# Two heads of a pair, matmul by matmul instead of head by head, in the scan of a two-block model

## The reference, cut to what matters

```python
a_cs = jnp.cumsum(a, axis=-1)
seg = a_cs[..., :, None] - a_cs[..., None, :]
decay = jnp.where(causal, jnp.exp(jnp.where(causal, seg, 0.0)), 0.0)
cb = jnp.einsum("bclgn,bcsgn->bcgls", cc, bc)
y_diag = jnp.einsum("bcgrls,bcsgrp->bclgrp", cb[:, :, :, None] * decay, xs)
...
y_off = jnp.einsum("bclgn,bcgrpn,bcgrl->bclgrp", cc, prev, jnp.exp(a_cs))
return (y_diag + y_off).reshape(b, t, h, p)
```

## Time and profile before

| what | value |
|---|---|
| median of three runs | 2549.59 us (2546.25 to 2555.57) |
| span of the profiled execution, the only time that its page gives | 2546.4 us |
| PE busy in the span | 2278.3 us (89%) |
| DVE busy | 1397.0 us (55%) |
| ACT busy | 1016.5 us (40%) |
| POOL busy | 949.7 us (37%) |
| the scan loop, four turns | 206 to 500 us of the span |
| one turn of it | 73.4 to 73.6 us |

### The profile page before, as it was taken

How to read it: one execution, slowest core, us unless ns; L and a number is a source line. 1 busy time by engine, 2 the same in 40 slices (tenths; PEclk the granted TensorE clock), 3 DMA queues, 4 the chain that set the end, 5 groups by cost and what they waited for, 6 DMA issues and landing times.

```text
span 2546.4 us, 34303 instructions
## 1 busy us (share of the span) xinstructions
PE 2278.3 (89%) x12362; PEld 1939.2 (76%) x12362; DVE 1397.0 (55%) x1514; ACT 1016.5 (40%) x1391; POOL 949.7 (37%) x253
## 2 busy tenths in 40 slices
PE   5998898878779799999789889999988988999996
PEld 3786676756658588878589879999988876778875
DVE  5637888899966433431355556306426565740633
ACT  4455555553252455542435533313223353331331
POOL 2333234336524144455432134343434223434431
PEclk9999999989889799999899889999999989999998
DMA  3232222211112122224221112222222111122221
GB/s 121 88 109 79 91 77 92 74 66 66 67 65 94 38 99 99 99 101 145 85 86 49 36 67 84 83 88 94 83 95 75 50 50 67 67 99 99 83 99 49
DMA packets 34492, 207.44 MB, mean 81 GB/s; under 512 B 4802, under 2 KB 4802, under 8 KB 10980
## 3 DMA queue, kind: packets, MB, share of 16 engines
q1 hardware_dynamic: 28128, 194.66, 21.7%
q10 hardware_dynamic: 6276, 11.57, 1.4%
HBM read 204.05 MB, written 2.17 MB: 81 GB/s over the span
## 4 chain that ended last, share of the span: by engine, by line
PE 64%; DVE 18%; DVEq 8%; ACT 4%; issue 3%; POOL 2%; ACTq 1%; DMA 0%; POOLq 0%
PE PS L505 20%; PE PS L507 19%; PE PS L509 19%; DVE vout L1578 5%; DVEq L1571 4%; POOL wlo L430 1%; PE PS L820 1%; DVEq L1474 1%; DVE hres L1475 1%; PE PS L846 1%; ACT whi L914 1%; DVE zres L1473 1%; DVE rstd L1465 1%; DVE rl L1966 1%; DVEq L1594 1%
## 5 line engine op out<-in xcount | busy, mean ns | idle before, releaser
L430 POOL TENSOR_TENSOR wlo<-raw,whi 128x2048 fp32r<-128x2048 f32 x181 | 842.2, 4653 | 1416.7 <-ACT whi L914 1398.9
L505 PE MATMUL PS<-ahi,whi 128*128 128x512 f32 (+1 forms) x2472 | 764.9, 350 | 89.4 <-DVE alo L1459 39.0
L507 PE MATMUL PS<-alo,whi 128*128 128x512 f32 (+1 forms) x2472 | 750.5, 344 | 0.0
L509 PE MATMUL PS<-ahi,wlo 128*128 128x512 f32 (+1 forms) x2472 | 748.2, 343 | 0.0
L914 ACT ACTIVATE whi<-raw 128x2048 fp32r<-128x2048 f32 x179 | 342.8, 1915 | 660.7 <-PE PS L509 655.3
L505 PEld LDWEIGHTS PS<-ahi,whi 128*128 128x128 f32 x2472 | 434.8, 193 | 165.8 <-issue 87.7
L507 PEld LDWEIGHTS PS<-alo,whi 128*128 128x128 f32 x2472 | 434.4, 192 | 52.5 <-issue 2.0
L509 PEld LDWEIGHTS PS<-ahi,wlo 128*128 128x128 f32 x2472 | 433.4, 192 | 52.6
L1578 DVE SCALAR_TENSOR_TENSOR vout<-vpad,cols,vout (+1 forms) x216 | 272.0, 1281 | 32.2 <-issue 31.6
L1966 DVE TENSOR_TENSOR rl<-rl,rstd 128x528 f32<-128x528 f32 (+1 forms) x64 | 149.0, 2328 | 248.3 <-ACT rl L1353 247.5
L505 PE MATMUL PS<-f2hi,whi 128*128 128x264 f32 (+1 forms) x768 | 205.9, 322 | 2.0 <-DVE f2lo L1972 1.8
(11 more groups left out here) (250 smaller groups left out, 2811.2 us busy)
## 6 DMA issues: line engine op xcount, KB each, us to landing
raw<-weights SPq DMA_DIRECT2D x181, 1024.0 KB, 4.8
acs_b<-acs_rows ACTq DMA_DIRECT2D x34, 256.0 KB, 3.2
const<-const ACTq DMA_DIRECT2D x2, 1232.0 KB, 6.0
x_in<-x_t SPq DMA_DIRECT2D x4, 512.0 KB, 5.2
out_t<-hres SPq DMA_DIRECT2D x8, 256.0 KB, 2.0
cols<-columns SPq DMA_DIRECT2D x1, 385.0 KB, 6.6
const<-const SPq DMA_DIRECT2D x1, 256.0 KB, 6.7
acs_rows<-dtt ACTq DMA_DIRECT2D x1, 64.0 KB
```

The lines of the kernel that those rows point to most:

```text
L430: nc.gpsimd.tensor_tensor(wlo[s][:, :], raw[s][:, :], whi[s][:, :].bitcast(F32), ALU.subtract).then_inc(lo_ready, 1)
L505: nc.tensor.matmul(o, wh, h, start=first, stop=False)
L507: nc.tensor.matmul(o, wh, h, start=False, stop=False)
L509: mm = nc.tensor.matmul(out[j], wl, hi[j], start=False, stop=last)
```

## The change: what it does

On PE, the two heads of a pair are issued together. There is one wait for `mc_ok` of both heads ahead of the pair, then for each chunk the own-chunk matmul of head 0, that of head 1, and the state matmuls of head 0 and of head 1. Both `y_mm` counts come at the end of the pair, one with the last matmul of each head. The matmuls are the same 14 per pair; their operands, places and accumulation are unchanged, and no other engine's program is changed.

```diff
-                def head(q):
-                    j, hh = q // 2, q % 2
-                    if hh == 0:
-                        hold(pe, y_ok, g * GP + max(j - 1, 0), "pe")
-                    hold(pe, mc_ok, g * GH + (q + 1), "pe")
+                def head_pair(j):
+                    hold(pe, y_ok, g * GP + max(j - 1, 0), "pe")
+                    hold(pe, mc_ok, g * GH + 2 * (j + 1), "pe")
+
+                    def out(hh, c):
+                        return PS[64 * hh:64 * hh + 64, (j % 2) * 512 + c * P:(j % 2) * 512 + (c + 1) * P]
+
+                    def cols_of(t, hh, c):
+                        q = 2 * j + hh
+                        return t[:, c * T + q * 64:c * T + q * 64 + 64]
+
                     for c in range(CHUNKS):
-                        o = PS[64 * hh:64 * hh + 64, (j % 2) * 512 + c * P:(j % 2) * 512 + (c + 1) * P]
-                        mm = nc.tensor.matmul(o, xdt[:, c * T + q * 64:c * T + q * 64 + 64],
-                                              m_slot[hh][:, c * P:(c + 1) * P], start=True, stop=(c == 0))
+                        cs = slice(c * P, (c + 1) * P)
+                        mm = [nc.tensor.matmul(out(hh, c), cols_of(xdt, hh, c), m_slot[hh][:, cs],
+                                               start=True, stop=(c == 0)) for hh in range(2)]
                         if c:
-                            mm = nc.tensor.matmul(o, st[:, (c - 1) * T + q * 64:(c - 1) * T + q * 64 + 64],
-                                                  c_slot[hh][:, c * P:(c + 1) * P], start=False, stop=True)
-                    mm.then_inc(y_mm, 1)
+                            mm = [nc.tensor.matmul(out(hh, c), cols_of(st, hh, c - 1), c_slot[hh][:, cs],
+                                                   start=False, stop=True) for hh in range(2)]
+                    for hh in range(2):
+                        mm[hh].then_inc(y_mm, 1)
...
-                head(0)
-                head(1)
+                head_pair(0)
                 z_glu(2, 0)
```

More of the change, by code:

```diff
@@ L712, in _ @@
                 hold(pe, st_ok, g + 1, "pe")
-                head(0)
-                head(1)
+                head_pair(0)
                 z_glu(2, 0)
-                head(2)
-                head(3)
+                head_pair(1)
                 z_glu(2, 1)
-                head(4)
-                head(5)
+                head_pair(2)
                 z_glu(3, 0)
-                head(6)
-                head(7)
+                head_pair(3)
                 z_glu(3, 1)
```

## The result

The changed kernel takes 2561.73 us (median of 6 runs, 2559.52 to 2565.18), against 2552.16 for the kernel before in the 6 runs by then (2546.25 to 2555.57). The ratio is 1.0046, with a 95% interval of 1.0030 to 1.0061: some 8 to 16 us slower (the two medians differ by 9.6 us). The prediction was 2557.4, from 2549 to 2566, within 0.5% most likely. The profiled span grew from 2546.4 to 2558.7 us.

What follows compares the result with a forecast made beforehand. Neither PE nor DVE is full; waits decide, along a chain from PE's head 0 over ACT to DVE. A + B + C = 1.95 us per turn, 7.8 over 4 turns: 2549.6 + 7.8 = 2557.4 us, case 2554 to 2561, range 2549 to 2566.

Steps and rivals of the forecast that it cites:

- What it can't save: Head 1's matmuls on PE already start when DVE's product is there; interleaving doesn't bring that operand earlier, removed waits are free.
- Length of a pair: An interleaved pair's 28 records on PE start 0.061 us apart, over 1.65 us, 0.21 more than head 1 alone.
- parallel bound: A pair's two heads on PE run perfectly in parallel: its records start over 1.44 us, nothing added.
- rival 3: PE bounds the turn and pairs get shorter, 1.65 for 2.97 us: 21 us back, 2529 us; chance 0.03.
- Term A: Head 0 of the first pair is counted later, delaying DVE through ACT at head 3: 1.24 us per turn.
- term C: PE's clock falls in the longer gap ahead of the fourth pair, delaying the next turn's transposes: 0.5 us per turn.
- B: The fourth pair ends later and DVE waits for it in y_out: 0.21 us per turn, between 0 and 1.53.
- Carrying the sum to the end: DVE's chain goes on from the loop into the next stage, so all 7.8 us reach the final time.
- The third pair is covered: ACT's longer wait for the third pair at head(6), up to 3.5 us more, costs nothing; 4.0 us remain at head 7.
- Rival 1: The alternating matmuls on PE don't overlap: 4.5 us per turn, 18 in all, 2568 us; chance 0.08.
- Rival 2: PE's clock falls in every turn ahead of the fourth pair, costing 2.5 us per turn: 2565 us; chance 0.16.
- Rival 4: DVE's late product is made up by later waiting in the turn: time stays at 2549.6 us; chance 0.07.

## Why the prediction was right, and where its sizes were off

- **What it can't save** held. No pair ever found both products waiting: PE waited 16 times, now longer.
- **Length of a pair**: I took 0.061 per record from a moment of overlap and from eight small transposes. Measured at full clock 0.055, a span of 1.48 us, near the parallel bound of 1.44. The overlap rows of before held the steady pace already: starts at 308.46, 308.52, 308.57 and 308.62, and only the last of the eight distances, to 308.73, is 0.11, that of a head alone. I averaged it in, and the transposes were no floor for this. The 2.97 us that I took for a pair issued head by head was too long as well: PE's second pair before has its 28 starts within 2.62 us (307.10 to 309.72), since its heads overlap by four records each, so rival 3's gain was too large from the start. The Trainium skill's rule that a further column tile adds next to nothing to a pack's span (TensorE: Matmul & The Clock Gate, the section on packing small matmuls) agrees with the trace here: 28 records in 1.48, 14 in 1.44. The same section's sentence that weight loads overlap running matmuls only for different row groups is not borne out: both heads use all 128 rows, and their 28 records, each with a weight load, start within the same 1.48 us.
- **Term A**, the late count of head 0: its place was right, its size off by two. Forecast 1.24 us per turn; measured 1.9 to 2.7, 10 us in all (2.57, 1.82, 2.56 and 2.56 of listed wait, which is 9.5). The mechanism's own part was right: with the clock kept up, head 3 waits 1.11, near the 1.14 of the parallel bound. What I left out is that the first pair would run at the low clock. I priced the clock as term C behind the fourth pair alone; the first pair's gap also grew, from 1.8 to 2.99 us, about the gap that the earlier trace rows show to be enough in some turns, and its length stands in the chain through ACT. That is the step that failed: the term for the first pair's clock, put at nothing, measured 0.7 to 1.5 us per turn at head 2.
- **Terms B and C** together were forecast at 0.71 per turn and measured 0.8 in `y_out` (9.7 less 6.5, over 4 turns). The parts were not: B was nearly nothing (with the pair at full clock `y_out` waits 1.52 against 1.48), C nearly all. And C came by another way than I gave for it. I had it in PE's tail into the next turn's transposes, and there DVE waited no longer than before (0.36, 0.36 and 0.35 us in the last three turns, 0.35 before); the low clock is paid inside the fourth pair, in `y_out`. So the agreement of the sum is luck.
- **What the sum did not have** is the time that DVE loses beside POOL's `wlo`, some 1.2 us in the loop.
- **Carrying the sum to the end** was wrong too: of the 16 us by which the profiled execution was behind at the end of the loop, 3.7 came back later. The loop's cost, 14.4 us, is nearly twice the 7.8 of the forecast. That the time came out nearer than this is in part luck.
- **The third pair is covered** held: ACT waited 5.52 us for it and DVE not at all for heads 6 and 7.
- **Rival 1** (no overlap) is refuted. **Rival 2** (the clock) was right in that the level fell in every turn, at the fourth pair too, but not in its price: no turn lost 2.5 us there. **Rival 3** fell with the waits. **Rival 4** (the slip is absorbed) fell within the turn, where nothing made it up. The outcome lies just above my case's own 2554 to 2561, by a clock that I had put in a rival and at the wrong pair.

## What to carry to other kernels

Before two chains of small matmuls are interleaved, ask whether both operands are there when the matrix engine arrives, and who waits for the first chain alone: here nobody could use the shorter pair, and ACT and DVE paid for head 0's later count. A joined wait also makes one gap of two, and a gap that lowers the clock lengthens the very work that others wait for; if it must be, another pair of buffers behind it hides most of the cost, 10 us of about 12 here. And a sum of waits that equals the growth of the span proves little until the stages are measured one by one: here a part of the loop's loss was in no wait, and a part of it came back elsewhere.

## What was not expected of the hardware

- Two float32 matmul chains whose outputs go to PSUM partitions 0 to 63 and 64 to 127 run side by side, each at the full pace of one alone: 28 records started within 1.48 us, 14 alone need 1.44.
- Without interleaving in the program, PE reaches ahead only a little: with both operands there, the second head began at 319.05, 1.11 us into the first, and 28 starts took 2.6 us. The kernel before does the same with its separate waits, and there PE's records don't start in program order: in the second pair of the second turn own-chunk records of head 1 start at 308.52 and 308.62, between state records of head 0 (308.46, 308.57) that the program has ahead of them.
- The same gap of 3.0 us ahead of the first pair lowered the clock in all four turns of the changed kernel, but in one of four with only that pair interleaved. So the gap's length alone doesn't decide it.
- DVE's products slow down beside POOL's `wlo`, and by how much depends on which starts first: three `xds` products took 5.39 us where POOL started 0.97 us ahead of them and 6.32 where it started 0.10 us behind. Moving `y_out` to save a wait of 1.48 us per turn ran into this, and the turns stayed as long.
